# MLA attention: probabilities left unnormalised, their sums taken from ones beside the values, and the gate divided by them

## The reference

```python
logits = jnp.einsum('bhqd,bhkd->bhqk', qi, k) * scale        # q, k: 96 wide (64 + 32 rotated)
mask = s_idx[None, :] <= t_idx[:, None]
w = jax.nn.softmax(jnp.where(mask, logits, -jnp.inf), axis=-1)
o = jnp.einsum('bhqk,bhkd->bhqd', w, v)                      # v: 64 wide, 16 heads
...
o = o.transpose(0, 2, 1, 3).reshape(B, S, 1024) * jax.nn.silu(gate)
x = x + o @ w_out
```

## Time and profile before

| | us |
|---|---|
| median of 3 runs (lowest, highest) | 1423.04 (1421.67, 1424.39) |
| the profiled execution | 1416.19 |
| its span | 1414.4 |
| PE busy | 1370.4 (97%) |
| DVE busy | 769.4 (54%) |
| ACT busy | 617.2 (44%) |
| POOL busy | 272.9 (19%) |

### The profile page before, as it was taken

One profiled execution on the slowest core, in us unless ns is written; L12 is line 12 of the kernel. 1 busy time (PEld: TensorE's weight loads), 2 busy tenths in 40 slices (PEclk: granted clock), 3 DMA queues, 4 the chain that ended last, 5 costly groups with the idle time before them and its releaser, 6 DMA issues.

```text
span 1414.4 us, 18397 instructions
## 1 busy us (share of the span) xinstructions
PE 1370.4 (97%) x6486; PEld 1114.4 (79%) x6486; DVE 769.4 (54%) x1271; ACT 617.2 (44%) x1100; POOL 272.9 (19%) x309
## 2 busy tenths in 40 slices
PE   6999999999999998999999999799999999999997
PEld 6888677788888887888888887688888888867776
DVE  5454788653652235787436436734665345347734
ACT  4347767434433326896235332123343333244534
POOL 3104733000000007672000005700000000324310
PEclk9999999999999999999999999899999999989998
DMA  5413000123232221002333332232333322310011
GB/s 155 134 51 121 31 0 0 45 90 98 81 105 100 94 90 60 0 0 88 106 91 99 123 91 88 74 90 63 90 104 112 96 97 71 112 42 0 1 45 60
DMA packets 54169, 106.10 MB, mean 75 GB/s; under 512 B 3460, under 2 KB 8280, under 8 KB 53720
## 3 DMA queue, kind: packets, MB, share of 16 engines
q1 hardware_dynamic: 52640, 98.91, 22.2%
q0 software_dynamic: 1376, 6.27, 1.5%
q10 hardware_dynamic: 88, 0.03, 0.0%
HBM read 103.11 MB, written 2.10 MB: 74 GB/s over the span
## 4 chain that ended last, share of the span: by engine, by line
PE 85%; DVE 6%; issue 5%; ACT 2%; DMA 1%; POOL 0%; DVEq 0%; POOLq 0%; SPq 0%; ACTq 0%
PE ps L421 21%; PE ps L423 21%; PE ps L422 21%; PE ps L569 3%; PE ps L798 2%; PE ps L593 2%; PE ps L816 2%; PE ps L701 2%; DVE w_lo L1379 1%; PE ps L582 1%; PE ps L799 1%; PE ps L691 1%; PE ps L762 1%; PE ps L692 1%; PE ps L550 1%
## 5 line engine op out<-in xcount | busy, mean ns | idle before, releaser
L1379 DVE TENSOR_TENSOR w_lo<-stage,w_hi 128x1024 fp32r<-128x1024 f32 (+4 forms) x188 | 238.3, 1267 | 491.9 <-ACT w_hi L906 491.8
L906 ACT ACTIVATE w_hi<-stage 128x1024 fp32r<-128x1024 f32 (+4 forms) x188 | 191.9, 1021 | 546.7 <-PE ps L423 546.6
L421 PE MATMUL ps<-a0h,w_hi 128*128 128x512 f32 x640 | 253.4, 396 | 10.1 <-DVE w_lo L1379 9.4
L423 PE MATMUL ps<-a0h,w_lo 128*128 128x512 f32 x640 | 250.7, 392 | 0.0
L422 PE MATMUL ps<-a0l,w_hi 128*128 128x512 f32 x640 | 250.5, 391 | 0.0
L421 PEld LDWEIGHTS ps<-a0h,w_hi 128*128 128x128 f32 x640 | 121.2, 189 | 37.5 <-DVE w_lo L1379 11.6
L423 PEld LDWEIGHTS ps<-a0h,w_lo 128*128 128x128 f32 x640 | 121.0, 189 | 25.7
L422 PEld LDWEIGHTS ps<-a0l,w_hi 128*128 128x128 f32 x640 | 121.3, 190 | 24.9 <-issue 0.2
L1906 POOL TENSOR_TENSOR small<-small 128x16 f32<-128x16 f32 (+2 forms) x15 | 33.4, 2224 | 535.8 <-DVE small L1457 396.1
L421 PE MATMUL ps<-w_hi,a0h 128*128 128x512 f32 (+1 forms) x320 | 122.2, 382 | 5.3 <-DVE w_lo L1379 5.3
L423 PE MATMUL ps<-w_hi,a0l 128*128 128x512 f32 (+1 forms) x320 | 120.5, 377 | 0.0
(11 more groups left out here) (272 smaller groups left out, 2557.8 us busy)
## 6 DMA issues: line engine op xcount, KB each, us to landing
stage<-in_a_w_in SPq DMA_DIRECT2D x48, 512.0 KB, 3.7
stage<-in_ple_w_gate SPq DMA_DIRECT2D x16, 512.0 KB, 3.3
stage<-in_w_kv_shared SPq DMA_DIRECT2D x16, 512.0 KB, 3.5
stage<-in_sb_w_in SPq DMA_DIRECT2D x16, 512.0 KB, 3.5
stage<-in_a_w_out SPq DMA_DIRECT2D x16, 512.0 KB, 3.3
stage<-in_b_w_in SPq DMA_DIRECT2D x16, 512.0 KB, 3.6
stage<-in_mla_w_in SPq DMA_DIRECT2D x8, 512.0 KB, 3.7
stage<-in_mla_w_out SPq DMA_DIRECT2D x8, 512.0 KB, 3.3
```

What stands on the lines that cost most here:

```text
L421: pe.matmul(bank, wh, mh, start=start, stop=False)
L423: return pe.matmul(bank, wl, mh, start=False, stop=stop)
L906: act.activation(w_hi[r % 2][:, 0:nk, 0:w], stage[r % 4][:, 0:nk, 0:w], ACT.Copy).then_inc(S("hi_ready"), 1)
L1379: dve.tensor_tensor(w_lo[r % 2][:, 0:nk, 0:w], stage[r % 4][:, 0:nk, 0:w], w_hi[r % 2][:, 0:nk, 0:w], ALU.subtract)\
```

## The change

`normalize` is gone, and so is the sum that ACT took with each exponential (`accum_out`). PE transposes the exponentials as they are and waits for `exp_done` where it waited for `p_ready`. `v_pair` is replaced by two tiles, `v_one[0]` and `v_one[1]`: in each, 64 columns hold one head's values and the other 64 hold ones, set once by POOL. So the product that gave the other head's useless rows now gives the sum of the exponentials in them, 64 times over. DVE (`o_recip`) takes the reciprocal of these 64 rows of 512 into `o_rec`; POOL (`over`) multiplies the head's gate by it, in place; and `o_gate`, as before, multiplies output and gate, after it has waited for POOL (`sg_over`).

```diff
-    v_pair = put("v_pair", [P, MB, P], 18)
+    v_one = [put("v_one0", [P, MB, P], 18), nc.alloc_sbuf_tensor_at("v_one1", [P, MB, P], F32, offset=SGM - 2048)]
+    o_rec = put("o_rec", [P, T], 0, of=SGM + 10 * 1024 - 2048)
...
-                pe.wait_ge(S("p_ready"), MB * h + (n + 1))
+                pe.wait_ge(S("exp_done"), MB * h + (n + 1))
...
-            pe.wait_ge(S("v_ok"), pair + 1)
+            pe.wait_ge(S("ones_v"), 2)
+            pe.wait_ge(S("v_ok"), 2 * pair + 2)
...
-                t = pe.matmul(ps[6][:, j * P:T], v_pair[:, j, :], prT[:, KEY_COL[j]:KEY_COL[j] + T - j * P],
+                t = pe.matmul(ps[6][:, j * P:T], v_one[s][:, j, :], prT[:, KEY_COL[j]:KEY_COL[j] + T - j * P],
...
-                               scale=scale, accum_out=ssum[:, j:j + 1]).then_inc(S("exp_done"), 1)
+                               scale=scale).then_inc(S("exp_done"), 1)
...
-            act.activation(v_pair[:, :, :].rearrange("p m (a d) -> p m a d", a=2), kv_tok[:, :, hs, HD:2 * HD], ACT.Copy)\
-               .then_inc(S("v_ok"), 1)
+            for s in range(2):
+                v = kv_tok[:, :, 2 * i + s, HD:2 * HD] if isinstance(i, int) else kv_tok[:, :, bass.ds(2 * i + s, 1), HD:2 * HD]
+                act.activation(v_one[s][:, :, head_rows(s)], v, ACT.Copy).then_inc(S("v_ok"), 1)
...
-        def normalize(h):
-            for r, j in enumerate(reversed(range(MB))):
-                dve.wait_ge(S("exp_done"), MB * h + (r + 1))
-                link(dve.reciprocal(rsum[:, j:j + 1], ssum[:, j:j + 1]))
-                at = slice(QRY_COL[j], QRY_COL[j] + (j + 1) * P)
-                dve.tensor_scalar(pr[:, at], pr[:, at], rsum[:, j:j + 1], None, ALU.mult).then_inc(S("p_ready"), 1)
+        def o_recip(h, s):
+            dve.wait_ge(S("o_done"), h + 1)
+            dve.wait_ge(S("sg_over"), h)
+            dve.reciprocal(o_rec[head_rows(s), :], ps[6][head_rows(s, True), :]).then_inc(S("rec_ok"), 1)
...
+        def over(h, s, pair):
+            pool.wait_ge(S("rec_ok"), h + 1)
+            g = sg[head_rows(s), pair, :] if isinstance(pair, int) else sg[head_rows(s), bass.ds(pair, 1), :]
+            pool.tensor_tensor(g, g, o_rec[head_rows(s), :], ALU.mult).then_inc(S("sg_over"), 1)
+            pool.wait_ge(S("sg_over"), h + 1)
...
+        pool.wait_ge(S("ring_used"), end_load("kv_up"))
+        for s in range(2):
+            pool.memset(v_one[s][:, :, head_rows(s, True)], 1.0).then_inc(S("ones_v"), 1)
...
+                pool.wait_ge(S("qk_ring"), 4 * i + 2 * s)
+                over(2 * i + (s - 4), s, i - 2)
                 mla_head(2 * i + s, s)
```

More of the change, by code:

```diff
@@ L584, in mla_probs_T, with mla_values @@
             t.then_inc(S("pT_done"), 1)
-        def mla_values(h, pair, first):
+        def mla_values(h, s, pair, first):
             pe.wait_ge(S("pT_a"), h + 1)
             pe.wait_ge(S("pT_b"), h + 1)
-            pe.wait_ge(S("v_ok"), pair + 1)
+            pe.wait_ge(S("ones_v"), 2)
+            pe.wait_ge(S("v_ok"), 2 * pair + 2)
             if not first:
@@ L603, in mla_pair @@
             if not first:
-                mla_values(a - 1, i - 1, False)
+                mla_values(a - 1, 1, i - 1, False)
             mla_k(b, 1)
@@ L609, in mla_pair @@
                 mla_q(a + 2, 0)
-            mla_values(a, i, first)
+            mla_values(a, 0, i, first)
             if not last:
@@ L655, in on_the_way @@
                 return {2: extra_inputs, 6: spatial_weights}
-            return {1: lambda: mla_values(HEADS - 1, PAIRS - 1, False), 2: extra_inputs}
+            return {1: lambda: mla_values(HEADS - 1, 1, PAIRS - 1, False), 2: extra_inputs}
         pe.wait_ge(S("pT_a"), HEADS)
@@ L1111, in mla_pair @@
                 act.wait_ge(S("o_done"), a)
-            hs = slice(2 * i, 2 * i + 2) if isinstance(i, int) else bass.ds(2 * i, 2)
-            act.activation(v_pair[:, :, :].rearrange("p m (a d) -> p m a d", a=2), kv_tok[:, :, hs, HD:2 * HD], ACT.Copy)\
-               .then_inc(S("v_ok"), 1)
+            for s in range(2):
+                v = kv_tok[:, :, 2 * i + s, HD:2 * HD] if isinstance(i, int) else kv_tok[:, :, bass.ds(2 * i + s, 1), HD:2 * HD]
+                act.activation(v_one[s][:, :, head_rows(s)], v, ACT.Copy).then_inc(S("v_ok"), 1)
             probs_T(a, first)
@@ L1653, in mla_pair @@
             maxima(a)
-            normalize(a)
             if not first:
+                o_recip(a - 1, 1)
+            probs_T(a, first)
+            if not first:
+                dve.wait_ge(S("sg_over"), a)
                 o_gate(a - 1, 1, i - 1, ps[6], "o_done", "o_read", "o_mla")
-            probs_T(a, first)
             maxima(b)
@@ L1662, in mla_pair @@
                 o_lo(i - 1, a0h, a0l, "o_mla")
-            normalize(b)
+            o_recip(a, 0)
+            probs_T(b)
+            dve.wait_ge(S("sg_over"), a + 1)
             o_gate(a, 0, i, ps[6], "o_done", "o_read", "o_mla")
-            probs_T(b)
         dve.wait_ge(S("sg_ready"), 8)
@@ L1669, in _ @@
         with dve.Fori(1, PAIRS - 1) as i:
-            link.begin(i, 1, 16)
+            link.begin(i, 1, 8)
             mla_pair(i)
@@ L1674, in _ @@
         split_to(lin["out0"].load0 + 1)
+        o_recip(HEADS - 1, 1)
+        dve.wait_ge(S("sg_over"), HEADS)
         o_gate(HEADS - 1, 1, PAIRS - 1, ps[6], "o_done", "o_read", "o_mla")
@@ L1975, in _ @@
             for s in range(2):
+                pool.wait_ge(S("qk_ring"), 4 * i + 2 * s)
+                over(2 * i + (s - 4), s, i - 2)
                 mla_head(2 * i + s, s)
         link.end(PAIRS - 2)
+        pool.wait_ge(S("qk_ring"), 2 * HEADS)
+        for h in range(HEADS - 4, HEADS):
+            over(h, h % 2, h // 2)
         root(nrm, MB, "nrm_in", 2, "nrm_ok")
```

## The result

The changed kernel takes **1439.3 us** (median of 4 runs, 1438.6 to 1440.2) against 1422.4 for the kernel before (4 runs, 1419.6 to 1424.4): a ratio of 1.013, with a 95% interval of 1.0106 to 1.0155. It is slower by 17 us. Its profiled execution took 1439.0 us, the span is 1437.2.

A forecast was written before the change was run, and what follows sets the result against it. PE was taken to bound the kernel at 6.94 us a head, with DVE close behind; DVE would need 4.36 + 3.6 + 0.42 = 8.38 and become the bound, adding 20 us to 1423.0: 1443 us, range 1434 to 1462.

The forecast's parts named there:

- The step that decided the sign: DVE's 64x512 reciprocal: two tiny ones, 157 and 178 ns, read as 7 ns an element, hence 3.6 us a head.
- the lower bound of 4 ns: Reciprocal's cost an element by the nearest pair of single instructions (165 and 177 ns), making it 2.2 us.
- half the split: On DVE, half of the split of a pair of heads, put at 0.31 us a head.
- its wait: DVE standing at the gate for POOL's product, with two semaphore hops, less the copies: 0.42 us a head (0 to 0.8).
- the maxima: DVE's maxima of a head, start to start, taken as unchanged at 2.40 us.
- Start and end: Attention stage's ends: maxima of head 2 end 1.8 us late; at the last heads 0.2 us is won.
- The sum: Attention stage: 1.8 us at the start, 18.7 over thirteen heads, less 0.2 at the end, 20 us slower.
- One element a cycle: Rival: reciprocal takes 0.68 us like the product, PE stays the bound, 1422 to 1423.5 us; chance 0.10.
- Slower still: Rival: reciprocal takes eight or nine cycles an element, 4.3 to 4.7 us; 1454, up to 1462 us; chance 0.08.
- the main case: Forecast as summed: DVE bounds at 8.38 us a head with PE's clock full, 1443 us; chance 0.70.
- the fear: Rival: PE's clock falls to half in the attention stage as PE idles; 1467 us, or 1450 if once or twice; chance 0.12.
- My lower price for the case without POOL's wait: Reciprocal 3.35 us, product 0.75, no wait for POOL: ACT and PE's chain hold a head at 7.9 us; 1435.5 us.

The follow-up runs named there:

- copy: The changed kernel with a plain copy in place of DVE's reciprocal, so the output is multiplied by the sums: 1423.2 us.
- half: The changed kernel with the reciprocal over 256 of the 512 columns and a copy over the other 256: 1431.5 us.
- swap: The changed kernel with POOL making the next head's q and k before it multiplies the gate by the reciprocal: 1451.0 us.
- nop: The changed kernel without POOL's product of gate and reciprocal, so the output is not divided: 1433.0 us.
- clear: The changed kernel with reciprocal on ACT, output multiplied by it on DVE, then by gate on POOL after maxima scaling; high and low parts moved later: 1413.9 us.
- twice: The changed kernel with DVE's reciprocal made twice for each head, the result unchanged: 1516.7 us.

## Why the prediction was right, and where it was not

**What bounds it.** PE set the pace, with DVE close behind, and the reciprocal turned that round: both shown, by the windows of the changed kernel and by `copy`, `half` and the changed kernel in a row (6.94 or so, 7.7, 8.66 us a head for a first link of 0.69, 2.17 and 3.36 us). The step that decided the sign was the reading of two tiny reciprocals as a slope of 7 ns an element. It is 6.26. The sign would have held at the lower bound of 4 ns as well, but barely (2.2 us, where it turns at 2); that three elements gave the slope of 511 this well is luck in part. The product on POOL was put at 1.28 us and took 1.267.

**The terms of the sum.** The head was put at 8.38 us and took 8.66. From the timeline of the whole round, of which one half is shown above, start to start: the reciprocal 3.40 with what stands around it (3.6 predicted); the copies 1.02 (1.00); half the split 0.36 (0.31); the gate 0.67 (0.65); its wait 0.60 (0.42); the maxima 2.66 (2.40). These make 8.7 us; the last heads are shorter. Two terms were mis-sized. The wait was, because I took 0.07 us for each semaphore hop, for which I showed no row, and they took 0.21 (reciprocal to product, 217.33 to 217.54) and 0.14 (product to gate, 218.81 to 218.95). The maxima were, for a reason I had not seen. I called the move of POOL's product ahead of the rotation harmless, since POOL has room. It has, but the rotation now runs beside DVE's maxima, and DVE's scaling of two SBUF operands waits out each POOL instruction: `swap`, `nop` and `clear` bring it back to 150 ns. The Trainium skill states the rule ("SBUF — State Buffer", Who interferes with whom): a VectorE instruction with two SBUF inputs contends with a GpSimd instruction that reads SBUF, and the later one blocks until the other is through. The rows agree to 0.02 us, and the instructions of DVE that read one operand from PSUM, the maxima and the gate, kept their lengths (1.14 and 0.69 us).

**Start and end.** The maxima of head 2 begin 0.9 us later than before (1.8 predicted): the first head's maxima are 0.4 earlier and the reciprocal is short. From the maxima of head 15 to the transposes of `p_tok` it is 13.4 us instead of 13.8, so 0.4 won, for 0.2. The last values waited 0.8 us for the gate as foreseen, and the last split cost nothing.

**The sum.** 0.9 + 22.4 - 0.4 = 22.9 us in the profiled executions, where 20 was forecast; 17 between the medians. The 1443 us were too high by 3.7 although the stage lost more than I said: I added the stage's loss to the median of the kernel before, and that median is of the group with the lower clock, some 7 us longer, and the changed kernel's executions are not. Two errors, 3 us and 7, ran against each other, so that the number came this near is luck in part; the mechanism is not. The step that failed is "on the median of 1423.0, which is 6.9 above it, I put the same 20 us". From the profiled execution I had 1436, too low by 3.0, which is the stage's own error. Two smaller figures do not come out as written, and nothing rests on them: DVE's idle time in the earlier trace rows is 1.84 us of 15, not 1.9, and nine cycles an element would be 4.9 us, not 4.7.

**The rivals.** One element a cycle (0.68 us) is refuted by the row of the reciprocal. Of the two readings of the Trainium skill's pages, the repeat count of 8 gave 4.4 us and the chain over eight slices 0.7; the row, at 3.36 us, agrees with neither, and is nearer to the first. "Slower still" fell with it. The clock stayed at 1.00 in the stage, as the main case had it, and `twice` shows that the fear was not idle: it came once PE had gaps of nearly five microseconds. My lower price for the case without POOL's wait, 7.9 us a head, is what `nop` measured (7.89), but the reason that I gave holds by halves: in one head DVE waits 0.5 to 0.6 us for PE's values, in the next it is busy throughout.

**In the profile.** PE busy 79% in the stretch (82% said), DVE nearly without idle time but for the gate's wait, clock 1.00: as said.

## What to carry to other kernels

Price an operation by two sizes of it in the trace before it is made wide: a slope can hide in two tiny instructions, and dividing 512 numbers a row costs what five copies do. Before a product is moved behind a waiting engine, write the ring down, maxima to next maxima, with each engine's queue order in it: taking 3.36 us off the busiest engine gained nothing while the ring stayed, and taking POOL's product and the high and low parts out of the ring, on engines that kept all their work, gained all of it. An engine with idle time is no free place if what it does there shares a way to memory with the one that has none.

## What the runs showed of the hardware

- A reciprocal on DVE takes 157 ns for one element a row, 178 for four, 1746 for 256 and 3356 for 512: 6.26 ns an element. A copy of the same 64x512 takes 689 ns. ACT's logarithm and exponential over it take 591 and 629 ns, 1.22 us together.
- POOL's fp32 product of 64x512 takes 1.267 us, as long as one of 128x512 before (1.288): in this pair length counts, not rows.
- DVE instructions with two SBUF operands and POOL instructions that read SBUF excluded each other for the length of a whole instruction: a 0.15 us scaling became 0.52 and 0.84 us, a 0.69 us subtraction 1.12.
- With PE idle for up to 4.8 us in 14, the granted clock went down to half again and again; with waits of up to 1.3 us in 8.7 it stayed full. PE busy without a gap is no warrant for it either: in an execution of `copy` it was at half from 1311 to 1313 us, in a stage where that of the changed kernel stayed at 1.00, and a mean clock of 0.978 for 0.983 went with some 7 us of this kernel's time. What brings it down there no run shows.
